# Sums of squares by tokens in the layer norms of a two-block model

## The reference

```python
def _rmsnorm(x, g):
    xf = x.astype(jnp.float32)
    y = xf * lax.rsqrt(jnp.mean(xf * xf, axis=-1, keepdims=True) + EPS)
    return (y * g.astype(jnp.float32)).astype(x.dtype)

def _layernorm(x, g, b):
    xf = x.astype(jnp.float32)
    mu = jnp.mean(xf, -1, keepdims=True)
    var = jnp.mean(jnp.square(xf - mu), -1, keepdims=True)
    y = (xf - mu) * lax.rsqrt(var + LN_EPS) * g.astype(jnp.float32) + b.astype(jnp.float32)
    return y.astype(x.dtype)

def first_block(...):                  # 2 layers: attention mixer and squared-relu MLP
    ...
    h = _rmsnorm(h, norm_final)
    return h[:, N_META:]

def _layer(x, ...):                    # second block, 2 layers
    ...
    mix = jnp.einsum('bsd,de->bse', y, w_out)
    x = _layernorm(DEEPNORM_ALPHA * x + mix, ln1_g, ln1_b)
    ...
    x = _layernorm(DEEPNORM_ALPHA * x + ffn, ln2_g, ln2_b)
    return x
```

## Time and profile before

| | us |
|---|---|
| median of 3 runs | 4038.56 |
| lowest and highest | 4032.66, 4042.51 |
| the profiled execution | 4033.35 |
| its span | 4031.6 |

### The profile page before, as it was taken

One profiled execution on the slowest core, in us unless ns is written; L12 is line 12 of the kernel. 1 busy time (PEld: TensorE's weight loads), 2 busy tenths in 40 slices (PEclk: granted clock), 3 DMA queues, 4 the chain that ended last, 5 costly groups with the idle time before them and its releaser, 6 DMA issues. The chain is left out here.

```text
span 4031.6 us, 50607 instructions
## 1 busy us (share of the span) xinstructions
PE 3739.7 (93%) x20371; PEld 3088.7 (77%) x20371; DVE 1856.7 (46%) x2480; ACT 1199.0 (30%) x1746; POOL 172.5 (4%) x209
## 2 busy tenths in 40 slices
PE   7897999898999798999999899979899999989997
PEld 6756999876888585777888678858586788867885
DVE  5564524345534225266554543333526665454333
ACT  3353212234312134232233232224423223323222
POOL 0000000000000000001320000000000132000000
PEclk9898999988999898998999999989999899999998
DMA  3101222221222121221002122212122100212222
GB/s 115 57 1 53 94 90 89 84 47 43 102 94 94 67 84 42 84 84 42 1 6 105 63 94 99 90 63 84 42 84 84 42 1 6 105 63 94 99 88 84
DMA packets 49052, 278.93 MB, mean 69 GB/s; under 512 B 10255, under 2 KB 12817, under 8 KB 19481
## 3 DMA queue, kind: packets, MB, share of 16 engines
q1 hardware_dynamic: 48816, 275.89, 19.3%
q10 hardware_dynamic: 30, 0.17, 0.0%
HBM read 273.74 MB, written 2.27 MB: 68 GB/s over the span
## 5 line engine op out<-in xcount | busy, mean ns | idle before, releaser
L337 PE MATMUL ps<-xs,ffn_w 128*128 128x512 f32 x2112 | 483.5, 391 | 29.4 <-DVE xs L606 29.4
L337 PEld LDWEIGHTS ps<-xs,ffn_w 128*128 128x128 f32 x2112 | 399.2, 189 | 114.3 <-issue 31.0
L337 PE MATMUL ps<-u,mlp_w 128*128 128x264 f32 (+1 forms) x2880 | 457.3, 322 | 14.9 <-DVE mlp_w L600 10.2
L337 PEld LDWEIGHTS ps<-u,mlp_w 128*128 128x128 f32 x2880 | 418.3, 190 | 53.6 <-issue 15.7
L337 PE MATMUL ps<-hn,mlp_w 128*128 128x264 f32 (+1 forms) x2304 | 363.7, 320 | 0.0
L337 PEld LDWEIGHTS ps<-hn,mlp_w 128*128 128x128 f32 x2304 | 332.4, 188 | 30.4 <-issue 0.5
L337 PE MATMUL ps<-xs,cv_w 128*128 128x512 f32 x1152 | 277.6, 401 | 8.5 <-DVE cv_w L600 8.5
L337 PEld LDWEIGHTS ps<-xs,cv_w 128*128 128x128 f32 x1152 | 217.9, 190 | 75.0 <-issue 23.0
L337 PE MATMUL ps<-ff,ffn_w 128*128 128x512 f32 x1056 | 240.0, 389 | 0.0
L386 ACT CAST ffn_w<-raw 128x2048 fp32r<-128x2048 f32 (+1 forms) x74 | 124.1, 1677 | 383.2 <-PE ps L337 343.2
L337 PEld LDWEIGHTS ps<-ff,ffn_w 128*128 128x128 f32 x1056 | 198.2, 188 | 41.2
(11 more groups left out here) (411 smaller groups left out, 5092.8 us busy)
## 6 DMA issues: line engine op xcount, KB each, us to landing
raw<-in_w_ffn_up SPq DMA_DIRECT2D x44, 1024.0 KB, 4.7
raw<-in_w_up SPq DMA_DIRECT2D x32, 1024.0 KB, 4.8
raw<-in_w_down SPq DMA_DIRECT2D x32, 1024.0 KB, 4.8
raw<-in_w_conv SPq DMA_DIRECT2D x24, 1024.0 KB, 4.8
raw<-in_w_ffn_down SPq DMA_DIRECT2D x32, 704.0 KB, 4.1
raw<-in_w_mqk SPq DMA_DIRECT2D x10, 1024.0 KB, 5.0
raw<-in_w_qk_even SPq DMA_DIRECT2D x9, 1024.0 KB, 4.8
raw<-in_w_mv SPq DMA_DIRECT2D x8, 1024.0 KB, 4.8
```

Of the source, the lines that this page charges most:

```text
L337: ins = nc.tensor.matmul(bank(u)[:, h, :], w[:, s, wp, k * g.bw + j * P:k * g.bw + (j + 1) * P], g.xs[:, xp, k, h * n:(h + 1) * n], start= ...
```

## The change

`norm` loses the parameters and branches that its five calls don't use, and takes `ident`, the 128x128 identity. The squares of a chunk become the stationary operand, in four blocks of 128 tokens, and one column of the ones moves: the result is one column of PSUM for each block, [128 tokens, 1], accumulated over the eight chunks, in banks 0 to 3. Root and reciprocal run on [128, 4, 1]. PE then brings the inverses back to all partitions as [128, 512] in bank 5: for each block a matmul with the column broadcast over 128 columns as stationary operand and the identity moving. DVE's scaling reads that bank. The sum of `total` moves to bank 6. The number of elements in the squares, the centring, the scaling and the bias is unchanged, as is the number of square slots.

```diff
--- before.py
+++ after.py
@@ -679,124 +679,67 @@
                     low(nc.gpsimd, c)
 
 
-def norm(nc, ps, name, x, chunks, per_group, ones, mean, eps, gain_of, out=None, xs=None, total=None, bias_of=None):
-
-
-
-
-
-
-    n = x.shape[2]
-    halves = 1 if n <= 512 else 2
-    w = n // halves
-    groups = chunks // per_group
+def norm(nc, ps, name, x, out, ones, ident, mean, eps, gain_of, total=None, bias_of=None):
+
+
+    chunks, n = x.shape[1], x.shape[2]
+    blocks = n // P
     SQ = 4
-    NB = 3
     with stage(nc, name) as st:
         sq = st.sb("sq", [P, SQ, n])
-        inv = st.sb("inv", [P, 2, n])
+        inv = st.sb("inv", [P, blocks, 1])
         eps_col = st.sb("eps_col", [P, 1])
-        if out is None:
-            out = st.sb("normed", [P, chunks, n])
         scaled_to = x if bias_of else out
-        eps_set, mean_sum, centred = st.sem("eps_set"), st.sem("mean_sum"), st.sem("centred")
-        sq_ready, summed, root, inverse = (st.sem(k) for k in ("sq_ready", "summed", "root", "inverse"))
-        scaled, biased, high_done = st.sem("scaled"), st.sem("biased"), st.sem("high_done")
-
-        def pair(b):
-            return ps[:, 2 * b:2 * b + halves, 0:w]
-
-        def in_halves(ap):
-            return ap.rearrange("p (h n) -> p h n", h=halves)
-
-        def low(eng, c):
-            eng.wait_ge(high_done, c + 1)
-            eng.tensor_tensor(xs[:, 1, c, :], out[:, c, :], xs[:, 0, c, :].bitcast(F32), ALU.subtract)
-
-        def of(g):
-            return range(g * per_group, (g + 1) * per_group)
+        mean_bank, sums, inv_bank = ps[:, 6, 0:n], ps[:, 0:blocks, 0:1], ps[:, 5, 0:n]
+        eps_set, mean_sum, centred, sq_ready, summed, root, inverse, spread, scaled = (
+            st.sem(k) for k in ("eps_set", "mean_sum", "centred", "sq_ready", "summed", "root", "inverse", "spread", "scaled"))
 
         with nc.Block() as block:
             @block.tensor
             def _(pe):
-                def ones_times(b, data, start, stop):
-                    for h in range(halves):
-                        ins = nc.tensor.matmul(pair(b)[:, h, :], ones, data[:, h * w:(h + 1) * w], start=start, stop=stop)
-                    return ins
-
                 if total is not None:
-                    ones_times(NB, total, True, True).then_inc(mean_sum, 1)
-                for g in range(groups):
-                    if g >= NB:
-                        pe.wait_ge(root, g - NB + 1)
-                    for c in of(g):
-                        pe.wait_ge(sq_ready, c + 1)
-                        ones_times(g % NB, sq[:, c % SQ, :], c == of(g)[0], c == of(g)[-1]).then_inc(summed, 1)
+                    nc.tensor.matmul(mean_bank, ones, total, start=True, stop=True).then_inc(mean_sum, 1)
+                for c in range(chunks):
+                    pe.wait_ge(sq_ready, c + 1)
+                    for t in range(blocks):
+                        ins = nc.tensor.matmul(sums[:, t, :], sq[:, c % SQ, t * P:(t + 1) * P], ones[:, 0:1], start=(c == 0),
+                                               stop=(c == chunks - 1))
+                    ins.then_inc(summed, 1)
+                pe.wait_ge(inverse, 1)
+                for t in range(blocks):
+                    ins = nc.tensor.matmul(inv_bank[:, t * P:(t + 1) * P], inv[:, t, :].to_broadcast([P, P]), ident, start=True, stop=True)
+                ins.then_inc(spread, 1)
 
             @block.scalar
             def _(act):
-                def squares(g):
-                    for c in of(g):
-                        if total is not None:
-                            act.wait_ge(centred, c + 1)
-                        if c >= SQ:
-                            act.wait_ge(summed, c - SQ + 1)
-                        nc.scalar.activation(sq[:, c % SQ, :], x[:, c, :], ACT.Square).then_inc(sq_ready, 1)
-
-                def roots(g):
-                    if g == 0:
-                        act.wait_ge(eps_set, 1)
-                    act.wait_ge(summed, (g + 1) * per_group)
-                    if g >= 2:
-                        act.wait_ge(scaled, (g - 1) * per_group)
-                    nc.scalar.activation(in_halves(inv[:, g % 2, :]), pair(g % NB), ACT.Sqrt, bias=eps_col[:, 0:1],
-                                         scale=mean).then_inc(root, 1)
-
-                def finish(g):
-                    for c in of(g):
-                        if bias_of or xs is not None:
-                            act.wait_ge(scaled, c + 1)
-                        if bias_of:
-                            nc.scalar.activation(out[:, c, :], x[:, c, :], ACT.Identity, bias=bias_of(c)).then_inc(biased, 1)
-                        if xs is not None:
-                            if bias_of:
-                                act.wait_ge(biased, c + 1)
-                            nc.scalar.copy(xs[:, 0, c, :], out[:, c, :]).then_inc(high_done, 1)
-
-                for g in range(groups + 2):
-                    if g < groups:
-                        squares(g)
-                    if 1 <= g <= groups:
-                        roots(g - 1)
-                    if g >= 2:
-                        finish(g - 2)
+                for c in range(chunks):
+                    if total is not None:
+                        act.wait_ge(centred, c + 1)
+                    if c >= SQ:
+                        act.wait_ge(summed, c - SQ + 1)
+                    nc.scalar.activation(sq[:, c % SQ, :], x[:, c, :], ACT.Square).then_inc(sq_ready, 1)
+                act.wait_ge(eps_set, 1)
+                act.wait_ge(summed, chunks)
+                nc.scalar.activation(inv[:, :, :], sums, ACT.Sqrt, bias=eps_col[:, 0:1], scale=mean).then_inc(root, 1)
+                for c in range(chunks if bias_of else 0):
+                    act.wait_ge(scaled, c + 1)
+                    nc.scalar.activation(out[:, c, :], x[:, c, :], ACT.Identity, bias=bias_of(c))
 
             @block.vector
             def _(dve):
                 if total is not None:
                     dve.wait_ge(mean_sum, 1)
                     for c in range(chunks):
-                        nc.vector.scalar_tensor_tensor(in_halves(x[:, c, :]), pair(NB), -mean, in_halves(x[:, c, :]),
-                                                       ALU.mult, ALU.add).then_inc(centred, 1)
-                for g in range(groups + 1):
-                    if g < groups:
-                        dve.wait_ge(root, g + 1)
-                        nc.vector.reciprocal(inv[:, g % 2, :], inv[:, g % 2, :]).then_inc(inverse, 1)
-                        dve.wait_ge(inverse, g + 1)
-                        for c in of(g):
-                            nc.vector.scalar_tensor_tensor(scaled_to[:, c, :], x[:, c, :], gain_of(c), inv[:, g % 2, :],
-                                                           ALU.mult, ALU.mult).then_inc(scaled, 1)
-                    if g >= 1 and xs is not None:
-                        for c in of(g - 1):
-                            if c % 2:
-                                low(nc.vector, c)
+                        nc.vector.scalar_tensor_tensor(x[:, c, :], mean_bank, -mean, x[:, c, :], ALU.mult, ALU.add).then_inc(centred, 1)
+                dve.wait_ge(root, 1)
+                nc.vector.reciprocal(inv[:, :, :], inv[:, :, :]).then_inc(inverse, 1)
+                dve.wait_ge(spread, 1)
+                for c in range(chunks):
+                    nc.vector.scalar_tensor_tensor(scaled_to[:, c, :], x[:, c, :], gain_of(c), inv_bank, ALU.mult, ALU.mult).then_inc(scaled, 1)
 
             @block.gpsimd
             def _(pool):
                 nc.gpsimd.memset(eps_col[:, :], eps).then_inc(eps_set, 1)
-                if xs is not None:
-                    for c in range(0, chunks, 2):
-                        low(nc.gpsimd, c)
 
 
 def row_norm(nc, ps, name, x, chunks, groups, pick, place, mean, eps, gain_of, xs=None):
@@ -1840,7 +1783,7 @@
                        room=room, scratch=a["scratch"], sinks=sinks[:, :])
             with parts("u1", D_FF // 2 // P, SEQ) as u, parts("hn1", KC, SEQ) as hn1:
                 after_mixer("mlp1", u[:, :, 0:KC, :], mix, u, hn1, SEQ, 1, real, 1)
-        norm(nc, ps, "fin", real, KC, KC, ones, 1.0 / D, EPS, lambda c: par[:, 32 + c:33 + c], out=x2)
+        norm(nc, ps, "fin", real, x2, ones, ident, 1.0 / D, EPS, lambda c: par[:, 32 + c:33 + c])
 
 
 def blocks_of(w, bw):
@@ -2638,7 +2581,7 @@
             load_all(nc, "lp", [(par[:, :], a["par2"][bass.ds(layer, 1), :, :].rearrange("a p n -> (a p) n"))])
 
             def ln(name, buf, total, g, b):
-                norm(nc, ps, name, buf, KC, KC, ones, 1.0 / D, LN_EPS, lambda c: par[:, g + c:g + c + 1], out=x,
+                norm(nc, ps, name, buf, x, ones, ident, 1.0 / D, LN_EPS, lambda c: par[:, g + c:g + c + 1],
                      total=total, bias_of=lambda c: par[:, b + c:b + c + 1])
 
             ws.layer = layer
```

## The result

| | before | after |
|---|---|---|
| median of 15 runs, us | 4033.41 | 4042.39 |
| lowest and highest | 4022.92, 4042.51 | 4037.53, 4051.7 |
| span of the profiled execution | 4031.6 | 4040.6 |

The ratio is 1.0025, 95% interval 1.0015 to 1.0034: slower by a quarter of a percent, less than the 0.3% that the prediction takes as the least that can be told from no change, though with fifteen runs each the interval leaves out 1. The direction, the mechanism and the range held; of the forecast +11.9 us the medians show +9.0, the ratio +10, and the five norms in the two traces +12.6. The level was put 8 us too high (4050), 5 of them because the median of the three runs known then, 4038.56, was above that of all fifteen.

What follows compares the result with a forecast made beforehand. The norms were taken as uncovered chains that count 1:1 in the span: sums +20.1, root -2.5, reciprocal -15.9, spread +10.2, total +11.9 us on 4038.6, giving 4050 us; range 4032 to 4060 for 8 in 10.

Steps and rivals of the forecast that it cites:

- Sums: In each of five norms, 64 load-and-matmul records at 0.213 us a step, 13.90 us to ACT: +20.1 us in all.
- Clock: Granted clock during the new sums: 0.50 throughout all five norms, since even fewer columns move than at line 1165; chance 0.84.
- first pieces at 1.00: Start of a norm's sums, if the clock has not yet fallen: would save up to 1 to 2 us a norm.
- Root and reciprocal: From 512 to 4 elements a partition: root saves 0.50 us a norm, reciprocal 3.18; -2.5 and -15.9 in all.
- Spread: New PE step between reciprocal and scaling, four matmuls, fully exposed: +2.0 us a norm, +10.2 in all.
- Scaling from PSUM: DVE's scaling reads the inverse from PSUM: nothing gained or lost beyond 0.1 us.
- rival 3: Stages after the norms lose or gain the clock: 1 us a norm either sign, some 3 in all; no separate chance.
- Rival 1: Clock rises during the new sums as during the old: -13.9 us, 4025 us; chance 0.13, whole or in some norms.
- Rival 2: In the sums, the one-column matmul does not overlap the next load: +38 us more, 4089 us; chance 0.03.

Runs made afterwards that it cites:

- the last kernel: The kernel before, without the change, with squares and ones in the rounded float32 type and the root's table loaded early in layer norms: 4000.34 us, ratio 0.9904.

## Why the prediction came out as it did

*Sums.* Forecast +20.1 us; the stretches went from 49.4 in all to 69.5, +20.1. The step taken from line 1165, where 16 columns moved, carried over to one column to the third digit: 1.89 + 56 x 0.213 = 13.82 against 13.81 to 13.83. The step at full clock, 0.111, was 0.112 in the kernel with columns only in the first half.

*Clock.* Taken as 0.50 throughout, and it was, in all five. I had put this at 0.84 from one stretch of 11.5 us. That stretch moved 16 columns behind 128-column loads up to 206.7 us, and 32 columns behind 64-column loads after it, so it was a mixed neighbour and not a copy of the new sums. The run with 128 columns shows that the forecast's cause, few moving columns, was right for these sums, the one with 32 that a matmul behind each load is not enough. Part of the exactness is luck: the clock had fallen 0.6 to 2.6 us before each of the five sums, while in two of the other executions it was still at 1.00 when the sums between the halves began. The first pieces at 1.00 that the prediction kept in its range could have come. By the rule of the Trainium skill, page "TensorE: Matmul & The Clock Gate", section "Why this matters for your kernels", that a continuously busy TensorE gets the full clock, the sums after the change should have sped up; they were busy 13.80 of 13.80 us and did not. Here the measurement decides: in this kernel a busy PE was not enough, and in the rounded type not even 128 columns a record were.

*Root and reciprocal.* -2.5 and -15.9 forecast. The root is 0.26 instead of the 0.19 that I took from a copy of 32 columns, the reciprocal 0.18 as taken: -2.1 and -15.9. Alone, in the kernel before, they gave 3.56 a norm.

*Spread.* +2.0 a norm forecast, +2.13 measured (2.17 from the reciprocal's end to the first scaling, less 0.04 before): +10.7 in all for +10.2.

*Scaling from PSUM.* Nothing forecast; 5.36 against 5.39 us for eight.

The measured terms (+20.1, -2.1, -15.9, +10.7) add up to +12.8, and slightly shorter scalings and copies make it the +12.6 of the traces; the sum said +11.9. The two terms that were off are the root, 0.4 us too much saved in all, and the spread, 0.5 too little.

*The rest of the program.* Outside the norms the eleven traces have between 3916.6 and 3931.1 us for the same code, 3923.1 before and 3919.5 after. A single execution therefore says little below 10 us of span; the norms' own stretches and the medians do. Much of the scatter goes with the granted clock. From the norm between the halves to the first layer norm, where all eleven kernels have the same code, it was 898.1 us with the clock at 0.50 for 58 of them in the last kernel, and 909.0 with 86 in the one with the small root and reciprocal alone, and the other nine lie near one line between the two, within 1.3 us. That scatter, and the old sums' dependence on when the clock falls (7.1 to 10.2 us for the same sixteen records), is why the medians' +9.0 and the traces' +12.6 need not agree. It is not shown to be all: in each of the six kernels with a ratio, this change among them, the ratio stands for 2 to 10 us less than the norms of the traces account for. Where that lies is open. Of rival 3 only the next stage's unchanged start at 0.50 is shown.

*Chances.* "Within 0.3%" and "slower" had 0.45 each for a forecast on the line. A sum of +11.9 against a line at 12.1 could not decide between them, and the measured +10 fell just short of it. Rival 1 was not the case, but it named what a risen clock would be worth. Rival 2 (no overlap of load and short matmul) is refuted by the step of 0.213.

## What to carry to other kernels

Before turning a matmul round so that its result is small, count loads. The small operand saves columns only where something else than the load sets the step. Here one, 32 and 128 float32 columns behind a 128x128 load all took 0.213 us a record at clock 0.50. Then look at the granted clock and at what the engine moves while it works: 64 records a norm were free to carry 128 columns each, and doing so turned a ratio of 1.0025 into 0.9962. Try it on the kernel in question, since in the rounded type the same 128 columns did not bring the clock up. And ask first whether the sums need full float32 at all: one type for the squares brought more (0.9924, in the old order) than the whole reordering.

## What the runs showed that I had not expected

A PE that is busy 13.80 of 13.80 us with loads and one-column matmuls gets clock 0.50, and the same program with 128 columns a record gets 1.00 after 4.3 to 6.0 us; with 32 columns it does not. In the rounded type with 128 columns PE was busy for 7.06 us without a break and the clock stayed at 0.50 in all five norms. I had expected 0.50 there, but for a reason that was not the case, pauses of PE. A load of a 128x128 block of the rounded type takes the step of a plain float32 one, 0.213 us at 0.50, so the type halves the number of loads and not their length.
